# Token norms of a two-block network: sums of squares in quarters on four column groups, inverse root by GpSimd

## The reference, cut to what matters

```python
def layer_norm(x, g, b):
    mu = jnp.mean(xf, axis=-1, keepdims=True)
    var = jnp.mean(jnp.square(xf - mu), axis=-1, keepdims=True)
    y = (xf - mu) * lax.rsqrt(var + LN_EPS)
    return (y * g + b).astype(x.dtype)

def rms_norm_2(x, g):
    y = xf * lax.rsqrt(jnp.mean(xf * xf, axis=-1, keepdims=True) + RMS_EPS)
    return (y * g).astype(x.dtype)
...
x = layer_norm(ALPHA * x + 0.5 * swiglu(x, ffn1_w1, ffn1_w3, ffn1_w2), ln1_g, ln1_b)
...
x = layer_norm(ALPHA * x + merged @ w_out, ln2_g, ln2_b)
x = layer_norm(ALPHA * x + 0.5 * swiglu(x, ffn2_w1, ffn2_w3, ffn2_w2), ln3_g, ln3_b)
ple = jax.nn.sigmoid(x @ ple_w_gate) * (p @ ple_w_proj)
x = layer_norm(ALPHA * x + ple, ln4_g, ln4_b)
...
h = rms_norm_2(x, norm_g) * (1.0 + scale) + shift
```

## Time and profile before

| | |
|---|---|
| median of 3 runs | 3132.92 us (3130.56 to 3133.13) |
| the profiled execution | 3131.53 us, with a span of 3129.7 us |
| mean granted TensorE clock | 0.998 |
| PE busy | 3082.8 us, 98% of the span |
| PEld busy | 2490.4 us, 80% |
| DVE busy | 2368.0 us, 76% |
| ACT busy | 1222.6 us, 39% |
| POOL busy | 56.2 us, 2% |

### The profile page before, as it was taken

How to read it: one execution, slowest core, us unless ns; L and a number is a source line. 1 busy time by engine, 2 the same in 40 slices (tenths; PEclk the granted TensorE clock), 3 DMA queues, 4 the chain that set the end, 5 groups by cost and what they waited for, 6 DMA issues and landing times.

```text
span 3129.7 us, 37552 instructions
## 1 busy us (share of the span) xinstructions
PE 3082.8 (98%) x14712; PEld 2490.4 (80%) x14712; DVE 2368.0 (76%) x4017; ACT 1222.6 (39%) x1884; POOL 56.2 (2%) x49
## 2 busy tenths in 40 slices
PE   8999999999999999999999999999999999999998
PEld 6887888877988887777878888888777788788887
DVE  6777767778869678888598776767797789789736
ACT  4233323335342455554243233222366534534414
POOL 0000000000000001130000000000000000000000
PEclk9999999999999999999999999999999999999999
DMA  3222212223343351012212111111211221122242
GB/s 131 74 73 75 81 61 68 68 68 109 119 101 135 115 197 56 8 48 114 95 54 68 41 54 61 48 54 48 68 54 63 104 77 64 48 70 101 81 168 74
DMA packets 89247, 250.13 MB, mean 80 GB/s; under 512 B 8560, under 2 KB 24816, under 8 KB 87536
## 3 DMA queue, kind: packets, MB, share of 16 engines
q1 hardware_dynamic: 89072, 247.73, 23.5%
HBM read 203.65 MB, written 44.04 MB: 79 GB/s over the span
## 4 chain that ended last, share of the span: by engine, by line
PE 90%; DVE 7%; ACT 2%; issue 1%; DMA 0%; DVEq 0%; SPq 0%; ACTq 0%
PE PS L577 88%; PE PS L582 2%; DVE WS L2228 1%; DVE X L2236 1%; DVE XS L2236 1%; DVE HELD L2290 1%; DVE X L2228 1%; ACT XS L1345 0%; DVE COLB L3038 0%; DVE XSf L2228 0%; ACT XSf L1345 0%; DVE TMP L2228 0%; DMA RAW<-in_W 0%; DVE TMP L2232 0%; ACT WS L1345 0%
## 5 line engine op out<-in xcount | busy, mean ns | idle before, releaser
L577 PE MATMUL PS<-XS,WS 128*128 128x512 f32 (+1 forms) x6480 | 1513.8, 391 | 20.4 <-DVE XS L2228 9.5
L577 PEld LDWEIGHTS PS<-XS,WS 128*128 128x128 f32 x6480 | 1208.9, 188 | 297.8 <-issue 27.1
L577 PE MATMUL PS<-HS,WS 128*128 128x512 f32 x2208 | 511.0, 390 | 3.1 <-DVE TMP L2228 2.7
L577 PEld LDWEIGHTS PS<-HS,WS 128*128 128x128 f32 x2208 | 414.1, 188 | 93.1 <-DVE TMP L2228 3.5
L2228 DVE TENSOR_TENSOR WS<-RAW,WS 128x512 fp32r<-128x512 f32 (+1 forms) x398 | 346.9, 880 | 173.8 <-ACT WS L1345 173.2
L1345 ACT ACTIVATE WS<-RAW 128x512 fp32r<-128x512 f32 (+1 forms) x398 | 307.6, 779 | 398.7 <-PE PS L577 344.0
L2228 DVE TENSOR_TENSOR X<-PS,X 128x512 f32<-128x512 f32 x272 | 184.2, 688 | 101.8 <-PE PS L577 101.7
L2228 DVE TENSOR_TENSOR TMP<-TMP,PS 128x512 f32<-128x512 f32 x304 | 203.6, 682 | 61.5 <-PE PS L577 58.7
L577 PE MATMUL PS<-T,WS 128*128 128x512 f32 x960 | 230.6, 389 | 0.0
L577 PEld LDWEIGHTS PS<-T,WS 128*128 128x128 f32 x960 | 180.2, 188 | 37.4
L1345 ACT ACTIVATE TMP<-PS 128x512 f32<-128x512 f32 x144 | 85.0, 596 | 291.0 <-PE PS L577 274.4
(11 more groups left out here) (338 smaller groups left out, 3580.6 us busy)
## 6 DMA issues: line engine op xcount, KB each, us to landing
RAW<-in_W SPq DMA_DIRECT2D x263, 512.0 KB, 3.3
RAWX<-in_W SPq DMA_DIRECT2D x30, 512.0 KB, 3.3
DC<-TMP SPq DMA_DIRECT2D x32, 256.0 KB, 2.1
X<-in_xT SPq DMA_DIRECT2D x8, 512.0 KB, 8.9
DX<-X SPq DMA_DIRECT2D x2, 2048.0 KB, 8.4
DCZ<-CA SPq DMA_DIRECT2D x8, 512.0 KB, 4.1
DGA<-TMP SPq DMA_DIRECT2D x16, 256.0 KB, 2.3
DGB<-TMP SPq DMA_DIRECT2D x16, 256.0 KB, 3.1
```

Of the source, the lines that this page charges most:

```text
L577: done = d.matmul(out, l, r, start=first, stop=last)
```

## The change

- The means of squares: for every norm of the list above, and for all halves, TensorE takes each of the eight squared tiles in four products instead of one (or of the DVE's sum). Product g multiplies the quarter of 128 tokens by a 128x32 matrix of 1/1024 and writes PSUM partitions 32g to 32g+31, so the four stand in four column groups of the array, and the bank's first 128 columns hold all 512 tokens' means. `SUMMED` and DVE's seven additions go.
- The mean of a layer norm: the ones matrix becomes one of 1/1024, a single column read 128 times. DVE's scaling goes; DVE subtracts straight from the PSUM bank.
- The factor: ACT copies the 128x128 means out with epsilon added (`factor_slot`), GpSimd raises them to the power -0.5 in place (`rstd_rows`, a tensor_tensor with `pow`), TensorE spreads row 32g over all partitions with a column of the identity (`spread`, four fp32 products of 128x128), and ACT copies the bank of 128x512 to `HELD` or `HX` (`spread_copy`). ACT's square root over 512 columns and DVE's reciprocal go.
- Hooks: each norm has one piece more on TensorE, the spread, so `within` names more places (after tile 4, or after tiles 4 and 7). GpSimd does the two powers of ln1 ahead of its attention work and the other eight behind it.
- The buffer `VA` is declared one line earlier, with no effect on its place. The other norms of the kernel (over 256, 384, 512 features, the context's and the final one) stay as they were.

```diff
-SUMMED = ("ln1", 1), ("ln2", 0), ("ln2", 1), ("ln3", 1), ("ln4", 0)
...
+    SHARE, POWER = COLB[:, 318:319], COLB[:, 319:320]
...
+        def quarter_sums(out, src, first, last):
+
+            return mms([(out[32 * g:32 * g + 32, 0:128], SHARE.to_broadcast([128, 32]), src[:, 128 * g:128 * g + 128], first, last)
+                        for g in range(4)])
+
+        def spread(name, h):
+
+            r = tmp("rs", name, h)
+            e.wait_ge(po("rs", name, h), dma("const")("cols"))
+            mms([(var_bank(name, h)[:, 128 * g:128 * g + 128], ident[:, 32 * g:32 * g + 1].to_broadcast([128, 128]), r[:, 0:128], True, True)
+                 for g in range(4)]).then_inc(*mm.inc("rb", name, h))
...
-            if (name, h) in SUMMED:
-                yield
-                e.wait_ge(ve(name, "sqs", 7, h), *banks.free(var))
-                mms([(bank(*var), ones[:], squares(name, 0, h), True, True)]).then_inc(*mm.inc(name, "var", 7, h))
...
-                    mms([(bank(*var), ones[:], squares(name, k, h), k == 0, k == 7)]).then_inc(*mm.inc(name, "var", k, h))
-            yield
-            yield
+            for k in range(8):
+                if k == 4:
+                    yield
+                e.wait_ge(ac(name, "sq", k, h))
+                quarter_sums(bank(*var), squares(name, k, h), k == 0, k == 7).then_inc(*mm.inc(name, "var", k, h))
+            yield
+            spread(name, h)
             yield
...
-                product8(u, h, use, "mh", pair=mh_pair, beside=h == 1, within=m in (3, 6) and h == 1 or None)
+                product8(u, h, use, "mh", pair=mh_pair, beside=h == 1, within={3: (4,), 6: (4, 7)}.get(m) if h else None)
...
-                product8(us[m], h, use, "ln3", beside=True, within=n in (1, 2, 3, 8, 9, 10, 12) or None)
+                product8(us[m], h, use, "ln3", beside=True,
+                         within={1: (4,), 2: (4,), 3: (4, 7), 8: (4,), 9: (4,), 10: (4, 7), 12: (4, 7)}.get(n))
...
+        def factor_slot(name, h):
...
+            act(tmp(*use)[:, 0:128], var_bank(name, h)[:, 0:128], ACT.Identity, bias=EPS[RMS_EPS if name == "h" else LN_EPS]).then_inc(
+                *ac.inc("ms", name, h))
+
+        def spread_copy(name, h, *ready):
+
+            e.wait_ge(mm("rb", name, h), *ready)
+            act(factor(name, h), var_bank(name, h), ACT.Copy).then_inc(*ac.inc("rc", name, h))
...
-            ts(s, bank(name, "mean", h), 1.0 / 1024, None, ALU.mult).then_inc(*ve.inc(name, "mean", h))
...
-                for k in range(1, 8):
-                    e.wait_ge(ac(name, "sq", 0, h), ac(name, "sq", k, h), *([ve(name, "sqs", k - 1, h)] if k > 1 else ()))
-                    tt(total, total, squares(name, k, h), ALU.add).then_inc(*ve.inc(name, "sqs", k, h))
-            yield
-            e.wait_ge(ve(name, "c", 7, h))
-            rstd(name, h, s)
+                e.wait_ge(mm(name, "mean", h), ready(k, h))
+                tt(X[:, k, half(h)], src[:, k, half(h)], bank(name, "mean", h), ALU.subtract).then_inc(*ve.inc(name, "c", k, h))
...
+        def rstd_rows(name, h):
+
+            r = tmp("rs", name, h)[:, 0:128]
+            e.wait_ge(ac("ms", name, h), ve("power"))
+            d.tensor_tensor(r, r, POWER.to_broadcast([128, 128]), op=ALU.pow).then_inc(*po.inc("rs", name, h))
```

More of the change, by code:

```diff
@@ L481, in var_bank, with factor @@
         return bank(name, "var", h) if name in LNS else bank("sq", name, h)
+    def factor(name, h):
+        return HX[:, h, :] if name == "h" else HELD[:, h, :]
     def out_part(p):
@@ L593, in product8 @@
             for k in range(8):
-                if within and k == 4:
+                if within and k in within:
                     hook()
@@ L639, in merge_norm @@
             mean, var = ("ln2", "mean", h), ("ln2", "var", h)
-            banks.take(mean, (ve, "ln2", "mean", h))
-            e.wait_ge(ve("ones"), ve("ln2", "sum", 7, h), *banks.free(mean))
-            mms([(bank(*mean), ones[:], HELD[:, h, :], True, True)]).then_inc(*mm.inc(*mean))
+            banks.take(mean, (ve, "ln2", "c", 7, h))
+            e.wait_ge(ve("share"), ve("ln2", "sum", 7, h), *banks.free(mean))
+            mms([(bank(*mean), SHARE.to_broadcast([128, 128]), HELD[:, h, :], True, True)]).then_inc(*mm.inc(*mean))
             yield
-            banks.take(var, (ac, "rs", "ln2", h))
-            e.wait_ge(ve("ln2", "sqs", 7, h), *banks.free(var))
-            mms([(bank(*var), ones[:], squares("ln2", 0, h), True, True)]).then_inc(*mm.inc("ln2", "var", 7, h))
+            banks.take(var, (ac, "rc", "ln2", h))
+            e.wait_ge(*banks.free(var))
+            for k in range(8):
+                e.wait_ge(ac("ln2", "sq", k, h))
+                quarter_sums(bank(*var), squares("ln2", k, h), k == 0, k == 7).then_inc(*mm.inc("ln2", "var", k, h))
+            yield
+            spread("ln2", h)
             yield
@@ L1119, in norm_h @@
             steps = norm("ln4", h)
-            for _ in range(3):
+            for _ in range(4):
                 next(steps)
                 yield
-            square_sum("h", h, 8, lambda k: SQ[k][:])
+            use = ("sq", "h", h)
+            banks.take(use, (ac, "rc", "h", h))
+            e.wait_ge(*banks.free(use))
+            for k in range(8):
+                e.wait_ge(ac("sq", "h", h, k))
+                quarter_sums(bank(*use), SQ[k], k == 0, k == 7).then_inc(*mm.inc("sq", "h", h, k))
+            yield
+            spread("h", h)
             yield
@@ L1963, in embed @@
             gate(10)
+            hook()
             h_squares(0)
@@ L2061, in mixer @@
                     halves()
-                    next(ln4)
+                    for _ in range(2):
+                        next(ln4)
                     h_squares(1)
                     biased(1)
-                    root("h", 1, 1024, RMS_EPS, mm("sq", "h", 1, 7))
+                    factor_slot("h", 1)
+                    spread_copy("h", 1)
                     for k in range(8):
@@ L3149, in part @@
                     ALU.add, ALU.subtract).then_inc(*ve.inc("xs", "h", k, h))
-            rstd("h", h, HX[:, h, :])
             for k in range(8):
-                e.wait_ge(ve("gc", 1), ve("rs", "h", h), ac("ln4", "y", k, h), *tmps.free(("hp", h, k)))
-                stt(tmp("hp", h, k), X[:, k, half(h)], GC[:, 0, k:k + 1], HX[:, h, :], ALU.mult, ALU.mult).then_inc(
+                e.wait_ge(ve("gc", 1), ac("rc", "h", h), ac("ln4", "y", k, h), *tmps.free(("hp", h, k)))
+                stt(tmp("hp", h, k), X[:, k, half(h)], GC[:, 0, k:k + 1], factor("h", h), ALU.mult, ALU.mult).then_inc(
                     *ve.inc("hy", k, h))
@@ L3560, in vector @@
         d.memset(ones[:], 1.0).then_inc(*ve.inc("ones"))
+        d.memset(SHARE, 1.0 / 1024).then_inc(*ve.inc("share"))
+        d.memset(POWER, -0.5).then_inc(*ve.inc("power"))
         d.memset(EPS[LN_EPS], LN_EPS).then_inc(*ve.inc("eps0"))
@@ L3617, in split_low @@
                             op=ALU.subtract).then_inc(*pool_lo.inc(u))
+        def rstd_rows(name, h):
+            r = tmp("rs", name, h)[:, 0:128]
+            e.wait_ge(ac("ms", name, h), ve("power"))
+            d.tensor_tensor(r, r, POWER.to_broadcast([128, 128]), op=ALU.pow).then_inc(*po.inc("rs", name, h))
         assert len(pool_units) == len(POOL_SPLITS)
+        for h in range(2):
+            rstd_rows("ln1", h)
         for n in range(64):
@@ L3630, in gpsimd @@
                     split_low(j)
+        for name, h in (("ln2", 0), ("ln2", 1), ("ln3", 0), ("ln3", 1), ("ln4", 0), ("h", 0), ("ln4", 1), ("h", 1)):
+            rstd_rows(name, h)
         for ct in range(1, 4):
```

41 lines of the change are left out of this document (18 added, 23 removed).

## The result

The changed kernel takes 3326.4 us (median of 4 runs, 3326.25 to 3326.61) against 3132.9 before, a ratio of 1.062 with a 95% interval of 1.0605 to 1.0634: 193.5 us slower, where 8.9 us faster had been forecast. Its profiled execution has a span of 3324.8 us, 195.1 more than before.

A forecast was written before the change was run, and what follows sets the result against it. TensorE, busy 98% of the span, was taken to bound the kernel; -6.5 us of its work and -2.4 of waits gave -8.9, so 3124.0 us, with its own range 3118 to 3129 and 3117 to 3142 over all.

The forecast's parts named there:

- Part 2: Chain from last square product to spread: power taken as 1.3 us, between 0.33 and 3.3; waits where ACT is not free.
- rival 2: Slow power at ten places between sum and spread: at 3.3 us total +7, 3140; 25%.
- price per further us: Cost over the kernel of each further us of power above 1.5 us: some 8 us.
- break-even of 2.4 us: Length of GpSimd's power from which its cost cancels the whole gain.
- Part 1: TensorE's own work at the norms: small products, block entry and spreads added, ones products removed, -6.5 us in sum.
- rival 1: Square blocks on TensorE: passes in order, 0.44 us per tile, +17.5 us, total +6.6, 3139.5; 15%.
- the reading on passes: Strict product order applied to fp32 passes: a second pass holds back the next group's first, tile 0.44 us.
- ScalarE's blockers: ACT not free in three places; in half 0 of h eight bias additions, 5.0 us, make TensorE wait 2.7 us.
- The waits of 0.8: TensorE waiting for the late factor in ln3 half 0 and h half 1, 0.8 us each.
- Part 3: Existing TensorE waits beside norms shrink: ln1 by 1.9 and 0.6, ln2 half 1 by 2.1, ln3 half 1 by 1.3.
- Rival 3: DVE's relief is worth nothing and TensorE's gaps stay: -3.0 us, 3130; 15%.
- announced signs of failure: A square block over 1.8 us, a power over 2.4, or TensorE's gaps beside ln1 and ln2 remaining.

The follow-up runs named there:

- half_cols: Changed kernel with GpSimd's power over 64 of the 128 columns only, a straight line for the other 64: 3229.3 us.
- line: Changed kernel with GpSimd's power replaced by a straight line, one multiply and add over 128x128: 3118.7 us.
- early: `keep5` with ScalarE's root in half 0 of h after two of eight bias additions, and the spread copy before the last two: 3112.8 us.
- turned: Changed kernel with TensorE turning the means into columns, so the power covers 4 columns instead of 128: 3132.1 us.
- root128: Changed kernel with ScalarE's square root and VectorE's reciprocal over 128 columns in place of copy and power: 3126.3 us.
- keep5: `root128` with the five summed halves back on VectorE's sum, one product, root and reciprocal over 512 columns: 3117.4 us.
- sum5: `root128` with VectorE adding the squares first in the five summed halves, TensorE taking that sum in four small products: 3123.9 us.

## Why the prediction was wrong

**The step that failed** is the size of the power in Part 2. It was taken as 1.3 us, with 3.3 us as the upper end of its range; it is 20.8, six times that upper end. TensorE stood for nearly all of it at ten places, 193.4 us. The end rested on VectorE's factor of 5 between reciprocal and scaling, doubled: what a reciprocal costs on one engine turned out to say nothing about a power on another. The nearest row was near in engine and tile and not in kind of operation, and the text knew it ("a software function"), and still multiplied the measured row by four. With no row for an operation, an upper end that is a guess should have been carried as open.

**The mechanism was that of rival 2**, which had 25%, and its size was missed all the same, since it ended at 3140: "It costs at ten places, always between a sum and the spread that TensorE stands before." Its price per further us was put at 8 us over the kernel and is 10.2: (3326.4 - 3118.7) / (20.8 - 0.4). Of that 191.6 / 20.4 = 9.4 are waits, at all ten places alike, and 22.9 / 20.4 = 1.1 is the slow clock behind each wait (2.3 us at ln1 half 0), which was no term of the sum at all. Its break-even of 2.4 us counts the 8 us from the assumed 1.3; from the 1.5 that the text names it would be 2.6. No run tested it. An estimate from the runs: in `half_cols` GpSimd takes 10.8 us for line and power and TensorE waits 9.5, so 1.3 us are hidden; the gain of `line` without its own wait, 13.4 + 1.8 us over ten places, adds 1.5, which makes 2.8 us, if the clock stays up.

**The rest of the forecast held in direction and, by half, within 1.6 us.** The ledger, in us against the kernel before:

| half | forecast | `line` | changed kernel |
|---|---|---|---|
| ln1, 0 | -5.4 | -5.3 | +15.3 |
| ln1, 1 | +1.9 | +0.9 | +18.6 |
| ln2, 0 | +2.15 | +2.1 | +23.9 |
| ln2, 1 | 0 | -0.6 | +20.1 |
| ln3, 0 | -2.7 | -4.3 | +16.8 |
| ln3, 1 | +1.2 | +1.1 | +22.2 |
| ln4, 0 | +2.5 | +2.5 | +24.6 |
| h, 0 | -1.15 | -1.8 | +20.9 |
| ln4, 1 | -3.5 | -3.5 | +17.5 |
| h, 1 | -3.85 | -4.6 | +14.9 |
| elsewhere | 0 | +0.1 | +0.4 |
| all | -8.9 | -13.5 | +195.2 |

In `line`, +0.8 us before ln1 and -0.8 between ln1 and ln2 cancel in "elsewhere", where the two kernels do the same work; entries of that size aren't sure.

- *Part 1, TensorE's work.* Sixteen small products and the way in take 1.10 + 0.22 = 1.3 us (693.94 to 695.04 in `line`, and the twelve before in 2.94 instead of 2.72), forecast 1.2; with passes in order it would have been over 2. So the four column groups run at once and rival 1 is refuted. With it falls the reading on passes that the prediction tried on the strict order of start and end in the Trainium skill ("TensorE: Matmul & The Clock Gate", The mechanism). The spread takes 0.81 and 0.13 on the way in, 0.94 for 0.92.
- *Part 2, ScalarE's blockers.* Half 0 of h waits 1.8 us in `line`, forecast 2.7; GpSimd's instruction takes 0.3 us there instead of the 1.3 assumed, which covers the difference. The waits of 0.8 forecast for half 0 of ln3 and half 1 of h aren't there. That the eight bias additions are what makes the factor late was shown by `early`.
- *Part 3, the waits.* The mean of half 1 of ln1 starts 4.8 us earlier than in the earlier trace rows, 5.3 when the 0.5 us are counted by which `line` was late before ln1; forecast 5.4. Across the gaps behind ln2 half 1 and ln3 half 1 `line` gains 2.3 and 1.4 us, forecast 2.1 and 1.3. Half 1 of ln1 came out 1.0 us better than worked out, half 0 of ln3 1.6. Rival 3, relief worth nothing (-3.0), is refuted by `line`. `line` gains 4.6 us more than forecast. By the prediction's own working a power of 0.33 us instead of 1.3 takes some 4 us off, which is 3120 (the text has 3118 as its lower end, 2 us more than its terms give), so most of it is the short instruction in `line`; the rest was not settled beyond the table.

One of the three announced signs of failure, the power over 2.4 us, is what the first group of the profile shows; the other two, a block over 1.8 us and gaps that remain, did not come.

## What to carry to other kernels

Before a new operation stands between two TensorE products, give it a price from a row of the same operation on the same engine; where there is none, no multiple of a neighbour is an upper end, and the break-even (here 2.4 us, for 128 columns on an engine that needs 0.45 for a multiplication) is the number to weigh. In a row in order, a wait costs its length times the places where it stands, and the clock behind it on top: before a spread here, every wait of 4.0 us and more left the next products at half speed, and some of 2.2 to 3.8 us did. A change that gains in five places and loses in five should be split. Here root and reciprocal over 128 columns in place of the power, the new path only where eight products went, and the late factor moved ahead of work that nobody waits for made 0.65% faster out of 6% slower.

## What the runs showed of the hardware

- GpSimd's `pow` in fp32 costs 0.37 us and 0.159 us for each column, whatever the number of partitions (32, 64 or 128) and the exponent (1 or -0.5): 1.01 us for 4 columns, 20.7 for 128.
- In the changed kernel the first power takes 21.50 us, the fifth 21.06 and the other eight 20.72. This is no price of the power's first call: in `line`, without a power, the first instruction at that place takes 1.08 us and the fifth 0.65 against 0.30, 0.8 and 0.35 more as well, and in `turned` the first power of 4 columns takes 1.01 us like the others. What makes the two longer was not looked for. The Trainium skill ("GPSIMD Engine Reference", Instruction dispatch) gives about 6 us, with no instruction in the profile, for a first call to freshly loaded code. No such gap shows here: the first power starts 0.08 us after ScalarE's copy has ended.
- Fp32 products of 128x32 by 128x128 on four column groups: sixteen of them let the next product start after 1.0 to 1.1 us.
- TensorE's clock behind a wait, read from the spread: it takes 0.81 us with no wait (0.91 in a few places) and 0.91 after waits of 0.6 to 1.8 us, at full clock. After all twenty waits of 8.4 to 22.2 us (`half_cols`, the changed kernel) it takes 1.72 or 1.73, no more after 22.2 than after 8.4. In between the length alone doesn't decide: after 2.2 us at half 0 of ln3 it takes 1.72 in `root128` and 0.91 in `keep5`, `sum5` and `early`; after 3.8 us at half 0 of h it takes 0.91 in `root128`, with the three products behind it slower (1.03 instead of 0.78), and 1.73 in `sum5`; after 2.65 (`sum5`) and 4.04 (`keep5`) 1.73. What decides there no run shows. At ln1 the 48 products behind take 12.40 us after 19.4 of standing, instead of 11.00.
